# Products of the identity matrix in front of the last steps of a triangular inversion

## What is computed

```python
kk = jnp.einsum('nbhcd,nbhsd->nbhcs', kb, k) * decay
tmat = jnp.where(strict, kk, 0.0) + jnp.eye(c, dtype=q.dtype)
sol = lax.linalg.triangular_solve(tmat, rhs, left_side=True, lower=True, unit_diagonal=True)
```

## Time and profile before

| | |
|---|---|
| median of three runs | 1601.27 us (1598.33 to 1609.75) |
| the profiled execution's own time | 1615.54 us |
| its span, first to last instruction | 1613.8 us |
| TensorE busy | 1461.5 us (91%), 9414 matmuls |
| VectorE busy | 691.3 us (43%) |
| ScalarE busy | 355.4 us (22%) |
| mean granted clock of TensorE | 0.947 of 2.4 GHz |
| inversion, steps 0 to 31 | about 253 to 313 us of the span |

### The profile page before, as it was taken

One profiled execution on the slowest core, in us unless ns is written; L12 is line 12 of the kernel. 1 busy time (PEld: TensorE's weight loads), 2 busy tenths in 40 slices (PEclk: granted clock), 3 DMA queues, 4 the chain that ended last, 5 costly groups with the idle time before them and its releaser, 6 DMA issues. The chain is left out here.

```text
span 1613.8 us, 24656 instructions
## 1 busy us (share of the span) xinstructions
PE 1461.5 (91%) x9414; PEld 864.6 (54%) x9414; DVE 691.3 (43%) x1471; ACT 355.4 (22%) x744; POOL 249.7 (15%) x323
## 2 busy tenths in 40 slices
PE   8999888999898999897999877987999997979996
PEld 6788668887544444353545466863434342424442
DVE  3889747631533343342434258043233332323323
ACT  3766454220410111110111020132011111111111
POOL 5779525200100000000000000001000000000000
PEclk9999999799899999898999978987999998989999
DMA  7679361039389999999999881395999999999994
GB/s 271 208 189 258 129 162 55 2 132 367 142 339 419 423 423 422 425 422 424 420 422 423 365 301 72 129 384 188 363 423 425 422 425 423 423 423 420 426 422 192
DMA packets 101490, 512.46 MB, mean 318 GB/s; under 512 B 36836, under 2 KB 42020, under 8 KB 66300
## 3 DMA queue, kind: packets, MB, share of 16 engines
q1 hardware_dynamic: 91548, 481.81, 75.3%
q0 software_dynamic: 9824, 29.05, 4.9%
HBM read 508.92 MB, written 17.10 MB: 326 GB/s over the span
## 5 line engine op out<-in xcount | busy, mean ns | idle before, releaser
L1986 DVE TENSOR_TENSOR e_ac<-e_sl,banks 128x256 f32<-128x256 f32 x54 | 22.7, 421 | 408.5 <-ACT e_sl L1895 408.5
L1774 PE MATMUL banks<-upper,e_xgT 128*64 128x512 f32 (+1 forms) x864 | 195.5, 612 | 1.3 <-issue 1.1
L304 PE MATMUL banks<-hT,dense_ring 128*128 128x272 f32 x768 | 184.9, 399 | 5.3 <-DMA dense_ring<-in_w_in 5.3
L1381 POOL DMA_INDIRECT x_xg<-rows_dram,x_idx x54 | 53.6, 993 | 848.6 <-DVE x_idx L1373 842.2
L1774 PE MATMUL banks<-dense_ring,e_xgT 128*64 128x512 f32 (+1 forms) x320 | 149.5, 623 | 38.3 <-issue 37.2
L304 PEld LDWEIGHTS banks<-hT,dense_ring 128*128 128x128 f32 x768 | 147.5, 193 | 39.3 <-DMA dense_ring<-in_w_in 5.3
L1774 PE MATMUL banks<-experts,e_xgT 128*64 128x512 f32 (+1 forms) x704 | 153.4, 608 | 0.9 <-issue 0.9
L1774 PEld LDWEIGHTS banks<-dense_ring,e_xgT 128*64 128x64 f32 (+1 forms) x320 | 41.1, 131 | 134.5 <-issue 132.5
L1895 ACT ACTIVATE e_sl<-banks 128x256 f32<-128x256 f32 x54 | 20.8, 385 | 402.4 <-PE banks L1774 402.4
L1792 PE MATMUL banks<-x_sg,route_consts 128*128 128x272 f32 x432 | 104.5, 394 | 2.8 <-ACT route_consts L1910 1.4
L1774 PEld LDWEIGHTS banks<-upper,e_xgT 128*64 128x64 f32 (+1 forms) x864 | 65.1, 132 | 74.4 <-issue 74.4
(11 more groups left out here) (453 smaller groups left out, 2179.0 us busy)
## 6 DMA issues: line engine op xcount, KB each, us to landing
upper<-in_moe_gate_up SPq DMA_DIRECT2D x54, 2048.0 KB, 25.2
experts<-in_moe_gate_up SPq DMA_DIRECT2D x44, 2048.0 KB, 26.9
upper<-in_moe_down SPq DMA_DIRECT2D x44, 1024.0 KB, 25.2
experts<-in_moe_down SPq DMA_DIRECT2D x44, 1024.0 KB, 26.2
dense_ring<-in_moe_down SPq DMA_DIRECT2D x40, 1024.0 KB, 25.0
dense_ring<-in_moe_gate_up SPq DMA_DIRECT2D x20, 2048.0 KB, 15.0
dense_ring<-in_w_in SPq DMA_DIRECT2D x47, 512.0 KB, 4.6
x_gate_up<-in_moe_gate_up SPq DMA_DIRECT2D x10, 2048.0 KB, 19.2
```

The lines of the kernel that those rows point to most:

```text
L304: mm = pe.matmul(ps[g % 4][:, 0:T], slot[:, n % SLOTS_IN, c, :], hT[:, c, :], start=(c == 0), stop=(c == DC - 1))
L1381: pool.indirect_dma_start(out=ex["xg"][:, i % 2, :], out_offset=None, in_=mem["rows_dram"], in_offset=bass.IndirectOffsetOnAxis(ap=ex["idx ...
L1774: mm = pe.matmul(gub[e * n:(e + 1) * n, :], xgT[:, i % 2, c, e * n:(e + 1) * n], gate_up_weights(mem, j)[:, c, :], start=(c == 0), stop=(c ...
L1986: dve.tensor_tensor(ac[:], sl[:], gub[:, FF:], ALU.mult).then_inc(mul, 1)
```

## The change

In steps 20 to 31 of the inversion, behind the waits of `off_times_x(i)` and ahead of its own products, TensorE computes two products of the 128x128 identity with itself. They are written to columns 384 to 511 of the bank that the step uses, which no step reads. No semaphore is added or changed. By the condition `i >= 20` and the 32 entries of `work` these are 12 steps and 24 products.

```diff
+def keep_busy(pe, mem, out, times):
+
+
+    for _ in range(times):
+        pe.matmul(out, mem["ident"][:], mem["ident"][:], start=True, stop=True)
@@ off_times_x
                     if i >= 2:
 
                         pe.wait_ge(s_t1c, i - 1)
+                    if i >= 20:
+                        keep_busy(pe, mem, bank[i % 2][:, 3 * P:], 2)
                     for h in range(heads(s)):
                         cols = slice(h * w, (h + 1) * w)
                         out = bank[i % 2]
```

## The result

The changed kernel took 1614.26 us as the median of 20 runs (1609.05 to 1618.71). Over 20 runs of its own the kernel before came to 1609.47 us, and not to the 1601.27 of the three runs that the forecast started from. The ratio is 1.0031 with an interval of 1.0017 to 1.0046, that is 2.7 to 7.4 us slower, 5.0 in the middle. The forecast was +1.2 us and 1602.5 us, with a range up to 1612. The direction was right, the effect was four times as large as forecast, and the median that the range was built on was 8 us too low.

What follows compares the result with a forecast made beforehand. The prediction took TensorE to bound the inversion: added products, less the time saved by keeping 2.4 GHz, give +1.75 us, less 0.5 at the last product, +1.2 us on the 1601.27 median, so 1602.5 us, range 1596 to 1612.

Steps and rivals of the forecast that it cites:

- Keeping the clock gives back 12.6 - 7.0 = 5.6 us, and 0.5 at the last product, 6.1 in all: Inversion from products(25) to off_times_x(30), 12.6 us at low clock, runs faster at 2.4 GHz; the last product saves 0.5 us.
- the lay-out: The forecast's list of TensorE work from products(25) to off_times_x(30), repriced at high clock: 9.65 us including new products, against 12.6.
- A block costs 0.66 us at full clock: Steps 20 to 31: one step's added products cost 0.66 us at 2.4 GHz, seams included; lower bound 0.45.
- The sum at the place: Inversion's end: off_times_x(30) 1.75 us later, less 0.5 at the last product, gives +1.2 us, handed on one to one.
- TensorE is the bound of the steps, and the products lengthen its queue: Inversion: TensorE's groups follow without a wait, so the 24 added full products only make its queue longer.
- VectorE doesn't become the bound: Inversion steps: VectorE, 2.48 of 4.00 us busy in 304 to 308, keeps idle time and does not set the pace.
- The clock is kept through the steps: Steps 20 to 31: clock stays at 2.4 GHz; held through the steps but lost in the gap, chance 0.42.
- the rivals with a fall in the steps: Clock falls at products(25), 1611 us, chance 0.20; or between steps 28 and 30, 1606 us, chance 0.15.
- It falls in the gap, and `solve_rhs` runs at 1.2 GHz: Near-idle TensorE from 310.6 to 315.7 us loses the clock; 2.3 us in `solve_rhs` and first projection column not gained.
- The bare weight loads: Added products: loads not overlapped, 1.9 us a step instead of 0.66, +15 us, 1617 us; chance 0.02.
- Twelve steps: Inversion: the condition and 32 list entries give twelve steps with products; fifteen would add 2 us, chance 0.01.

Runs made afterwards that it cites:

- the three traces of before: The kernel before, unchanged, profiled three times; from step 19's 16x16 group to the start of `turn` it took 32.6, 29.5 and 32.7 us.
- the second profile of before: The kernel before, unchanged, profiled once more; from step 19's 16x16 group to the start of `turn` it took 29.5 us, the clock falling at 306.4 us.
- filling the gap: Changed kernel plus four products before the last step's product and five before `turn`; `solve_rhs` to `new_values(2)` took 5.6 us instead of 8.0.
- the four-step version: Kernel before plus two products only in steps 25, 28, 29, 31 and nine in the waits at the end; ratios 0.9946 (6 runs), 0.9985 (12).
- the nine products: Kernel before plus only four products before the last step's product and five before `turn`, none in steps 20 to 31; ratio 0.9996.
- the filled waits: Four identity products before the last step's product and five before `turn`, where TensorE waits; alone on the kernel before, ratio 0.9996.

## Why the prediction was wrong

*The number itself.* 1614.26 is 11.8 us above the forecast of 1602.5, and 8.2 of them are the start. Three runs of the kernel before had a median of 1601.27, twenty have 1609.47. I named that the profiled execution's 1615.54 stood 14 us above those three, and used the median all the same. From 1609.47 the forecast would have been 1610.7 with a range to about 1620, and the result would have lain inside. The other 3.6 us are in the effect, +4.8 between the medians instead of +1.2.

*Keeping the clock gives back 12.6 - 7.0 = 5.6 us, and 0.5 at the last product, 6.1 in all.* This is the step of the working that failed. It was read from one execution and taken for the kernel's. At `turn` the three traces of before lie 5.6, 2.5 and 5.7 us above TensorE's own work at full clock, the 27.0 us, 4.6 in the mean; 1.0 of the 2.5 is the wait for VectorE. The changed kernel lies 8.6 us above it in every trace. So the change pays 8.6 us to save 4.6, +4.0 at `turn`. The 6.1 was also 0.5 too much for the execution that it was read from: the lay-out priced the groups of eight in the joins at 0.41, and beside a block and an `outputs` one takes 308.57 - 307.97 = 0.60. Part of that is the block's own seam, so I can't say how much of the 0.5 it explains.

*A block costs 0.66 us at full clock.* The mechanism was right, the size was off: 0.79 between two middle steps, 0.78 over all. I took the seams from a block of 8 matmuls and measured only up to the next start. I left out the slow start inside the block (0.10) and the slower first group behind it (0.04). 11 x 0.12 is 1.3 us of the miss. The copy of step 30 shows both terms together: 314.79 - 284.04 = 30.75 us behind step 19's group against 309.25 - 281.93 = 27.32, so 3.4 later where 1.75 was forecast.

*The sum at the place.* The forecast's +1.2 us, plus 1.3 for the price of a block, plus 0.5 for a saving of 5.6 instead of 6.1 in the execution it was read from, plus 1.0 for the mean of 4.6 instead of that execution's 5.6, make the +4.0 at `turn`. Another 0.3 come behind it. `solve_rhs` takes 3.6 us at low clock in all six traces; but the clock comes back 0.4 to 1.1 us into the first projection column in the traces of before and 1.1 to 1.6 us into it in those of after. Together +4.3 us.

*TensorE is the bound of the steps, and the products lengthen its queue.* Right: dose and length go together from 1 to 8 products, and the whole follows.

*VectorE doesn't become the bound.* Right for the changed kernel, which has no such wait in the steps. For the bare steps at full clock it isn't, by the 1.04 us in the second profile of before.

*The clock is kept through the steps.* Right, three times of three, and the rivals with a fall in the steps (0.35 of the chances) did not come.

*It falls in the gap, and `solve_rhs` runs at 1.2 GHz.* Right: 0.229 a matmul in the profile after, and filling the gap gives 2.4 us back, where 2.3 was forecast.

*The bare weight loads* (1.9 us a step, 0.02): not so; a product inside a block costs 0.223 us, less than its two loads of 0.19 one after the other. Only the second matmul of a block comes 0.215 us behind the first, about the time of one load; that it waits for its load is not shown. *Twelve steps*: right, 96 instructions. A slip without effect on the sum: the page shows a 9 in slice 7, the dips are in slices 8 and 11.

What stays open: why the four-step version was 8.7 us below the kernel before in its first six runs. Its two profiled executions, 1599.46 and 1603.11 us, have the same A and B, so what sets them apart lies outside the place. Behind it the clock has further low stretches in the routing, from about 416 us on, whose length differs from one execution to the next (10.2 us in the first trace of before, 17.1 in the first of after); 2.6 us of the difference between those two executions arise there, between the norm's sums and the first gathered rows. No experiment was made on these stretches or on the wait for the gathered rows.

## What to carry to other kernels

Work that is there only to keep TensorE's clock up is paid in every execution, and what it saves depends on where the clock would have fallen in that execution: read the place in several profiles before pricing it. Try how few blocks hold it; here three or four did what twelve did, together with the filled waits. Put it where the engine waits, but only if the clock is still up there: at half clock the nine products took 4.4 us here and no longer fitted the waits. A median of three runs is not a base for an effect of 5 us when single runs lie 20 us apart.

## What was not expected of the hardware

- The clock fell at 296.5, 306.4 and 297.4 us in three executions of the same instructions, 14.6, 21.1 and 14.5 us behind the start of step 19. In the first and the third TensorE was busy throughout that time (14.50 of 14.50 us from 282 to 296.5, 14.40 of 14.40 from 283 to 297.4); in the second it waited once, the 1.04 us for VectorE. The Trainium skill, page "TensorE: Matmul & The Clock Gate", Part 1, ties the clock to how busy TensorE has been and names idle gaps as what brings it down; two traces show a fall without one.
- A block of full 128x128 products between 64x64 groups costs 0.34 us for the change of shape and the slow start, and 0.223 for each product. Small products in their place cost their own 0.47 us for 16 matmuls and nothing beside in step 24, more in the joins (0.55 in the mean of 11 blocks), and held the clock too, in one profile.
- Twelve blocks weren't needed: four of full products, one of them in a wait, with 0.45 us of products each, together with the filled waits held 1.00 in two profiles of two, and so did three blocks of small products in one. None of these was tried without the filled waits.
